# Suffix sums over key blocks taken as running sums on VectorE, with seven tail product pairs a head instead of ten, in a stick-breaking attention trunk

## The reference, cut to what matters

```python
def block(args):
    qi, i = args
    z = jnp.einsum('bhqd,bhkd->bhqk', qi, k).astype(jnp.float32) * scale
    q_pos = i * Q_BLOCK + jnp.arange(Q_BLOCK)
    strict = key_pos[None, :] < q_pos[:, None]
    log_1m = jnp.where(strict, jax.nn.log_sigmoid(-z), 0.0)
    tail = lax.cumsum(log_1m, axis=3, reverse=True) - log_1m
    a = jnp.where(strict, jnp.exp(jax.nn.log_sigmoid(z) + tail), 0.0)
    return jnp.einsum('bhqk,bhkd->bhqd', a.astype(v.dtype), v)
```

## Time and profile before

| | us |
|---|---|
| median of 3 runs | 760.4 (759.59 to 760.98) |
| the profiled execution's own time | 760.23 |
| its span, first to last instruction | 758.5 |

### The profile page before, as it was taken

How to read it: one execution, slowest core, us unless ns; L and a number is a source line. 1 busy time by engine, 2 the same in 40 slices (tenths; PEclk the granted TensorE clock), 3 DMA queues, 4 the chain that set the end, 5 groups by cost and what they waited for, 6 DMA issues and landing times.

```text
span 758.5 us, 9936 instructions
## 1 busy us (share of the span) xinstructions
PE 699.3 (92%) x3547; PEld 583.3 (77%) x3547; DVE 514.1 (68%) x563; ACT 413.8 (55%) x428; POOL 109.6 (14%) x112
## 2 busy tenths in 40 slices
PE   4999999979799999999999989999999999999920
PEld 3898888878688888888888948888888888888810
DVE  5878755665534326071544588999999999999927
ACT  6726675675442323131233337777777778777712
POOL 5000000000000000000000130333433443331120
PEclk9999999998899999999999999999999999999975
DMA  8552330000042232233476369999999999999444
GB/s 282 170 167 56 111 111 1 1 28 2 15 149 87 83 111 79 87 97 125 165 264 236 122 217 393 394 388 370 367 375 369 366 376 366 385 366 375 181 170 189
DMA packets 85169, 155.47 MB, mean 205 GB/s; under 512 B 6229, under 2 KB 37071, under 8 KB 84628
## 3 DMA queue, kind: packets, MB, share of 16 engines
q1 hardware_dynamic: 78452, 137.39, 51.2%
q0 software_dynamic: 6688, 17.69, 6.2%
HBM read 150.64 MB, written 12.58 MB: 215 GB/s over the span
## 4 chain that ended last, share of the span: by engine, by line
PE 83%; DVE 6%; ACT 5%; issue 3%; DMA 2%; POOL 1%; POOLq 0%; DVEq 0%; ACTq 0%
PE ps L481 24%; PE ps L482 24%; PE ps L483 24%; PE ps L1536 2%; PE ps L1276 1%; PE ps L1278 1%; DVE soft L1826 1%; PE ps L1593 1%; PE ps L1462 1%; PE ps L1562 1%; PE ps L1490 1%; DMA y_rows<-ye,y_col 1%; ACT log_in L911 1%; ACT log_in L909 1%; ACT soft_hi L917 1%
## 5 line engine op out<-in xcount | busy, mean ns | idle before, releaser
L454 DVE TENSOR_TENSOR ring_lo<-raw_a,ring_hi 128x2048 fp32r<-128x2048 f32 (+2 forms) x58 | 115.5, 1995 | 103.6 <-ACT ring_hi L448 103.6
L454 DVE TENSOR_TENSOR ring_lo<-raw,ring_hi 128x2048 fp32r<-128x2048 f32 x71 | 161.4, 2289 | 12.3 <-ACT ring_hi L448 11.0
L448 ACT ACTIVATE ring_hi<-raw 128x2048 fp32r<-128x2048 f32 x71 | 136.2, 1920 | 19.8 <-PE ps L483 19.8
L481 PE MATMUL ps<-hT_hi,ring_hi 128*128 128x512 f32 x288 | 114.3, 397 | 5.3 <-ACT attn L923 3.4
L448 ACT ACTIVATE ring_hi<-raw_a 128x2048 fp32r<-128x2048 f32 (+2 forms) x58 | 97.4, 1680 | 32.3 <-PE ps L483 32.3
L483 PE MATMUL ps<-hT_hi,ring_lo 128*128 128x512 f32 x288 | 113.1, 393 | 0.0
L482 PE MATMUL ps<-hT_lo,ring_hi 128*128 128x512 f32 x288 | 113.1, 393 | 0.0
L481 PE MATMUL ps<-ring_hi,xT_hi 128*128 128x512 f32 x240 | 94.8, 395 | 1.8 <-DVE xT_lo L2039 1.8
L483 PE MATMUL ps<-ring_hi,xT_lo 128*128 128x512 f32 x240 | 93.8, 391 | 0.0
L482 PE MATMUL ps<-ring_lo,xT_hi 128*128 128x512 f32 x240 | 93.7, 390 | 0.0
L481 PEld LDWEIGHTS ps<-hT_hi,ring_hi 128*128 128x128 f32 x288 | 54.6, 190 | 17.8 <-ACT attn L923 3.6
(11 more groups left out here) (347 smaller groups left out, 1230.4 us busy)
## 6 DMA issues: line engine op xcount, KB each, us to landing
raw<-in_w_down SPq DMA_DIRECT2D x25, 1024.0 KB
raw<-in_w_gate SPq DMA_DIRECT2D x47, 512.0 KB
raw<-in_w_up SPq DMA_DIRECT2D x47, 512.0 KB
raw_a<-in_w_in SPq DMA_DIRECT2D x15, 1024.0 KB
raw_a<-in_w_gate SPq DMA_DIRECT2D x17, 512.0 KB
raw_a<-in_w_up SPq DMA_DIRECT2D x17, 512.0 KB
raw_a<-in_w_down SPq DMA_DIRECT2D x7, 1024.0 KB
raw_a<-in_w_in SPq DMA_DIRECT2D x10, 512.0 KB, 7.5
```

What stands on the lines that cost most here:

```text
L448: act.activation(ring_hi[:, c[0] % SPLIT, 0:width], buf[:, 0:width], ACT.Copy).then_inc(hi_ready, 1)
L454: dve.tensor_tensor(ring_lo[:, s, 0:width], buf[:, 0:width], ring_hi[:, s, 0:width].bitcast(F32), ALU.subtract).then_inc(lo_ready, 1)
L481: pe.matmul(out_ap, l_hi, r_hi, start=start, stop=False, skip_group_check=True)
```

## The change

The suffix sum over key blocks is no longer made by products with ones. Behind `softplus(n)`, DVE adds the blocks up from the last to the first: block 2 takes block 3 (128 columns), block 1 takes block 2 (256), block 0 takes block 1 (384), each waiting for the one before (`link` puts a semaphore wait behind the instruction). With such running sums R, the tail of block s is triangle x R(s) + (ones - triangle) x R(s+1), so `tails` issues 4 + 3 = 7 pairs; the second matrix is `negrest`, and `negones` goes.

`log_in` goes, and `soft` and `soft_lo` are doubled, so the log is made in the buffer of the head's parity. The wait of `softplus` for the former head's tails and of `logarithm` for the former softplus goes; `soften` waits for the former head's tails instead. The order within a pair changes on all three engines: `softplus(2p+3)` is at the end of a pair on DVE, right behind `soft_low(2p+2)` and one projection's low part; the gate chunks are split in the middle of the next pair; `project_qk(5)` (24 matmuls of 512 columns) and `project_v(2)` (48 of 256) change places between `fill_a(0)` and `fill_b(0)`, and the first six of the 24 matmuls of `fill_b` go ahead of `values(2p+1)` (`CUT`). `values` of heads 6 and 7 go to banks 2 and 3, and the first gate to banks 6 and 7.

```diff
-    log_in = sb("log_in", [P, ZW], F32, "t", 0)
-    soft = sb("soft", [P, ZW], F32, "t", 5 * KB)
-    soft_lo = sb("soft_lo", [P, ZW], F32R, "t", 5 * KB)
+    soft = [sb(f"soft{b}", [P, ZW], F32, "t", 5 * b * KB) for b in range(2)]
+    soft_lo = [sb(f"soft_lo{b}", [P, ZW], F32R, "t", 5 * b * KB) for b in range(2)]
...
-    GATE_BANK = ((6, 2), (0, 1), (4, 5))
+    GATE_BANK = ((6, 7), (0, 1), (4, 5))
+
+    def value_bank(m):
+        return bank(7 if m < HEADS - 2 else m - 4)
...
                 act.wait_ge(z_ps, n + 1)
-                if n > 0:
-                    act.wait_ge(z_soft, n)
-                act.activation(log_in[:, :], scores(n), ACT.Abs).then_inc(act_c, 1)
+                buf = soft[n % 2]
+                act.activation(buf[:, :], scores(n), ACT.Abs).then_inc(act_c, 1)
...
             def soften(n):
                 act.wait_ge(z_soft, n + 1)
-                act.activation(soft_hi[:, :], soft[:, :], ACT.Copy).then_inc(soft_h, 1)
+                if n > 0:
+                    act.wait_ge(tail_ps, n)
+                act.activation(soft_hi[:, :], soft[n % 2][:, :], ACT.Copy).then_inc(soft_h, 1)
...
                 a, b = 2 * p, 2 * p + 1
+                soften(b)
                 weigh(a)
-                soften(b)
                 if p == 0:
-                    qk_hi(5, 6)
+                    v_hi_part(2, 6)
                 if p == 1:
                     qk_hi(6, 6)
+                    split_hi(act, K(C_MERGE))
                 if p == 2:
                     v_hi_part(3, 6)
+                    split_hi(act, K(C_MERGE + 1))
...
                 for sbk in range(TB):
-                    for jb in range(sbk, TB):
+                    for lhs, jb in ((negtri, sbk), (negrest, sbk + 1))[:TB - sbk]:
...
                 if p < HEADS // 2 - 1:
                     scores_pair(p + 1)
+                    fill_b(p, 0, CUT)
                 else:
-                    gate_part(KD // 2, KD).then_inc(chunk_used, 1)
+                    gate_half(0, 1, 0, None, 5, KD).then_inc(chunk_used, 1)
                 values(2 * p + 1)
-                fill_b(p)
+                if p < HEADS // 2 - 1:
+                    fill_b(p, CUT, KD)
...
+            dve.tensor_scalar(negrest[:, :], tri_f[:, :], -1.0, -1.0, ALU.mult, ALU.add).then_inc(consts_r, 1)
...
             def softplus(n):
                 dve.wait_ge(z_ln, n + 1)
-                if n >= 1:
-                    dve.wait_ge(tail_ps, n)
-                dve.scalar_tensor_tensor(soft[:, :], bank(3 * (n % 2), 3)[:, 0:ZW], 0.0, log_in[:, :],
-                                         ALU.max, ALU.add).then_inc(z_soft, 1)
+                buf = soft[n % 2]
+                link(dve.scalar_tensor_tensor(buf[:, :], bank(3 * (n % 2), 3)[:, 0:ZW], 0.0, buf[:, :],
+                                              ALU.max, ALU.add))
+                for sbk in (2, 1, 0):
+                    more = buf[:, ZOFF[sbk] + P:ZOFF[sbk] + ZN[sbk]]
+                    ins = dve.tensor_tensor(more, more, buf[:, ZOFF[sbk + 1]:ZOFF[sbk + 1] + ZN[sbk + 1]], ALU.add)
+                    if sbk > 0:
+                        link(ins)
+                ins.then_inc(z_soft, 1)
...
             cross_o(1)
             qk_lo(4, 6)
+            softplus(1)
             for p in range(HEADS // 2):
                 a, b = 2 * p, 2 * p + 1
-                softplus(b)
+                soft_low(b)
                 weight_hi(a)
-                soft_low(b)
                 weight_lo(a)
...
+                if p < HEADS // 2 - 1:
+                    softplus(b + 2)
                 value_lo(a)
                 value_lo(b)
```

More of the change, by code:

```diff
@@ L122, in build_trunk @@
     negtri = sb("negtri", [P, P], F32R, "const")
-    negones = sb("negones", [P, P], F32R, "const")
+    negrest = sb("negrest", [P, P], F32R, "const")
     rank_tri = sb("rank_tri", [P, P], BF16, "const")
@@ L954, in _ @@
                     soften(a + 2)
-                value_hi(a)
-                value_hi(b)
                 if p == 0:
-                    v_hi_part(2, 6)
+                    qk_hi(5, 6)
                 if p == 1:
@@ L962, in _ @@
                     logarithm(b + 2)
[L963 to L966, removed]
+                value_hi(a)
+                value_hi(b)
             act.preload_act_table_set("sigmoid_and_others")
@@ L974, in _ @@
                         after(act, K(C_MERGE + i, dp, PER_DP))
[L975 to L979, removed]
+                        act.activation(sig[:, i, :, :], gate_pair(i), ACT.Sigmoid).then_inc(g_sig, 1)
                 act.wait_ge(mg_ready, dp + 1)
@@ L1121, in _, with proj @@
                         ins.then_inc(hT_ps, 1)
-            def proj(b, wh, wl, o0, step):
-                for k in range(KD):
+            def proj(b, wh, wl, o0, step, k0=0, k1=KD):
+                for k in range(k0, k1):
                     o = o0 + k * step
@@ L1203, in cross_out, with project_qk @@
                 ins.then_inc(xo_ps, 1)
-            def project_qk(n, b):
+            def project_qk(n, b, k0=0, k1=KD):
                 wh, wl = chunk(K(C_PAIR[n // 2]))
-                proj(b, wh, wl, 1024 * (n % 2), P).then_inc(chunk_used if n % 2 else q_ps, 1)
+                ins = proj(b, wh, wl, 1024 * (n % 2), P, k0, k1)
+                if k1 == KD:
+                    ins.then_inc(chunk_used if n % 2 else q_ps, 1)
             def project_v(i, b):
@@ L1337, in _ @@
             project_qk(4, 6)
-            def gate_part(k0, k1):
-                wh, wl = chunk(K(C_MERGE))
-                for k in range(k0, k1):
-                    o = P + k * 256
-                    ins = three(pe, bank(GATE_BANK[0][1]), wh[:, o:o + P], wl[:, o:o + P], hT_hi[:, k, :], hT_lo[:, k, :],
-                                k == 0, k == KD - 1)
-                return ins
+            CUT = 2
             def fill_a(p):
@@ L1349, in fill_a @@
                     pe.wait_ge(qk_l, 5)
-                    project_qk(5, 6)
+                    project_v(2, 6)
                 if p == 1:
-                    pe.wait_ge(v_l, 3)
+                    pe.wait_ge(qk_l, 6)
                     project_qk(6, 6)
@@ L1798, in value_sum @@
                 dve.wait_ge(av_x, m + 1)
-                dve.tensor_tensor(sbT_f[rows, m // 2, :], bank(7)[rows, :], sbT_f[rows, m // 2, :], ALU.add).then_inc(av_sum, 1)
+                dve.tensor_tensor(sbT_f[rows, m // 2, :], value_bank(m)[rows, :], sbT_f[rows, m // 2, :], ALU.add).then_inc(av_sum, 1)
             cross_norm(0)
```

64 lines of the change are left out of this document (28 added, 36 removed).

## The result

The changed kernel takes 753.82 us (median of 5 runs, 751.12 to 755.46), beside 760.98 us (759.59 to 761.62) for the kernel before on the same chip: a ratio of 0.990 with a 95% interval of 0.987 to 0.993, that is 5.5 to 9.7 us less.

What follows compares the result with a forecast made beforehand. PE bounds the kernel (83% of the last chain), so a change counts where PE waits or its work shrinks. Full-clock savings of -9.8 us and +3.9 for clock falls give -5.9, 754.5 us; range 750.2 to 758.4.

Steps and rivals of the forecast that it cites:

- Tails and adds: Per head in the loop: tail products from 2.73 to 2.15 us; adds of 0.29, 0.42, 0.56 us, 1.35 with links.
- The chain: From z, the end of a pair's score products: first tails at 9.61 us; PE waits 2.9 there, 0.9 before second tails.
- The sum at full clock: Head loop without clock falls: -0.9 us before its first z, then +0.6, -5.5 and -4.0; together -9.8 us.
- The split: Gate chunk split in mid-pair (ACT 1.90, DVE 2.29 us) no longer holds up head 5; rival: something else does, chance 0.08.
- The fill ahead of the values: Six fill matmuls (1.38 us) before second head's values: only move the wait before first tails, yet cover late low weights.
- The clock: In the loop, three falls behind waits of about 2.9 us: net +3.8 to 3.9 us; rival: it stays up, chance 0.25.
- What is saved here moves everything behind it forward: Time saved in the head loop starts the following stage, full of PE work, earlier by the same amount.
- the prediction's own sign of being wrong: Among the signs named: the stage behind the head loop doesn't start earlier by the same amount.
- PEclk is below 1 in three stretches: Profile of the changed kernel: low TensorE clock in three stretches instead of two.

Runs made afterwards that it cites:

- e1: Changed kernel with its new order and buffers, but ten tail product pairs with ones and no adds: 748.73 us.
- e6: Changed kernel plus 20 products that nobody reads, in PE's wait before the first tails of each of three pairs: 752.82 us.
- e3: Changed kernel with both gate chunk splits put back at the end of the pair, behind the second head's logarithm: 764.16 us.
- e4: Kernel before with only the two gate chunk splits moved to the middle of their pair: 750.95 us.
- e2: Kernel before with the three adds, `negrest` and seven product pairs, in the old order with the old buffers: 767.78 us.
- e5: Changed kernel with all of `fill_b` behind the second head's values, none ahead of them: 753.27 us.
- e7: Changed kernel with a head's seven high-part products first, waiting for the high part alone, then the seven low-part ones: 752.12 us.
- r1: Changed kernel as it is, profiled a second time: 755.67 us in one run.
- e8: Changed kernel's order and buffers with ten product pairs, no adds, and the ten high-part products ahead of the ten low-part ones: 746.26 us.

## Why the prediction was right, and where it was not

754.5 was forecast, 753.82 came. The mechanism in the loop was right: the order gives, the sums take. That the total fits to 0.7 us is partly luck, as the last two points show. Step by step:

- **Tails and adds**: 2.15 us a head, and 0.291, 0.425, 0.560 us, as forecast. The rule of the Trainium skill, VectorE: DVE Perf Modes, section on the TRN2 errata, that each operation on SBUF pays a fixed latency, holds here: 128 columns took 0.291 us, not a third of the 0.560 that 384 took. Its cycle table gave 0.98 us for the three, an estimate, where they took 1.35 with their links. The same section says that this row of the table is too low, and for adds of this type gives 151 plus the columns, at 0.96 GHz; that is 0.291, 0.424 and 0.557 us, an estimate that these rows meet, and the prediction passed it over. (The second row is a copy, not an add; only the length of a link was taken from it.)
- **The chain**: tails 9.64 us behind z (forecast 9.61), PE idle 2.71 (forecast 2.9, though the forecast's own 9.61, less 6.8 of fills and values, is 2.8) and 0.63 (0.9). Right. e1's waits, 1.32 to 1.34, show that the adds are what makes the difference.
- **The sum at full clock**: e6 measures it. The first z in it is at 124.76, so -1.2 (forecast -0.9); then 24.57 us (24.7), 25.20 (24.7) and 25.84 (25.75), which is +0.5, -5.0 and -3.9. Together -9.6, where I had -9.8. The half microsecond above the forecast in the third period (25.20 for 24.7) stands beside a wait that I had not counted: there the values of head 4 wait 0.72 us for the low part of V, which DVE makes only after the low weights (170.44 in e6). e6 adds products to PE, but only where it waits.
- **The split**: e3 (+10.3 us) and e4 (-9.4 us) show that its place alone decides the sign of the change. That the split would have no price in the middle of the pair was right for ACT.
- **The fill ahead of the values**: "only moves this wait" was right. But I also had it cover the low weights of the second head, and said that PE would wait 1.4 us out without it. It does, and loses nothing, since it then waits that much less before the tails. The two sentences were one and the same 1.1 to 1.4 us.
- **The clock: mis-sized.** I charged three falls, behind the three waits of 2.9 us, the length of one at 5.2 us, 2.5 us each and +3.9 net. (The subtraction is off too: 2.5 less the 0.9 that is absorbed is 1.6, not 1.7.) The profile shows two falls of 3.41 us, one behind a 2.70 us wait and one behind the 2.18 before head 7. The third period is 25.81 us instead of e6's 25.20, and the last 27.26 instead of 25.84: +0.6 and +1.4, together the 2.05 us by which e6's loop ends earlier. Two things were off. First, "2.9 is nearer to 3.44 than to 0.79, so I let it fall three times": of twelve waits of 2.67 to 2.71 us in four profiles (the change, its two repeats, e3) five were followed by a fall. Around the waits of 3.4 to 6.3 us in the kernel before, e2 and e3 the clock was low each time. Behind shorter ones it fell at 1.66 (e4), 1.88 and 2.55 (e5), 1.98 and 2.33 (e2), 2.18 (the change), and in e7 at 1.18 with 0.27 behind it; it did not behind the three of 1.3 in e1, 1.55 in e5, 1.58, 1.58 and 1.65 in e2, 1.69 and 1.76 in e7 or 2.17 in e6. So no length parts the two cases up to 2.7 us; the chip's answer to the same wait differs from one execution to the next. Second, a fall costs less than its loss on PE, as the next wait absorbs it: in both repeats the fall behind the third 2.71 us wait left the last period at 25.8 us, because the wait for head 7 shrank from 2.17 to 0.6. That one I had nearly right, with 0.2. The Trainium skill, TensorE: Matmul & The Clock Gate, section on HAM oscillation, describes a loop whose waits of about 3 to 5 us bring the low clock back every time. The waits of 2.7 us here are shorter and brought it back in 5 of 12 cases, so that section did not bear out three falls, as the prediction has it.
- **"What is saved here moves everything behind it forward": failed.** By the prediction's own sign of being wrong, the stage behind the loop had to start earlier by the same amount; it starts 7.6 us earlier and the span is 6.1 us shorter, for the stage took 550.0 us where it had taken 548.5. In the thirteen profiles it lasts 548.3 to 548.6 us without a low stretch, 550.0 to 550.4 with one of 3.41 us, 551.9 with one of 6.83, and 553.2 to 553.6 with both, so 1.6 to 1.7 us for each 3.41. So -9.6 at full clock, +2.0 for the falls in the loop and +1.5 behind it make the -6.1 of the profiled span; I had +3.9 for the first and nothing for the second, and these nearly cancelled. That PEclk is below 1 in three stretches, as forecast, is luck in the same way: two lie in the loop and the third behind it.

**What stays open.** A stretch that begins between 409 and 413 us (at 420 in e3) stands in all seven profiles of kernels with the sums in the new order, and in none of the other six. PE is recorded fully busy there, in kernels with and without the stretch, and the 32 products of 20 columns stand at that place or just ahead of it in all of them. The second stretch behind the loop in r1 and e6, at 447 us, comes with a wait of 1.80 and 1.85 us on PE; the other eleven profiles have the same wait, 1.46 to 1.86 us, without one. The time at which the stage starts does not decide it alone: e4 starts it at 200.59 us without one, e6 and e7 at 200.37 and 200.30 with. Nor do the two groups of kernels surely part. Two of e1's six runs, of which there is no trace, took 752.45 and 753.32 us at a mean granted clock of 0.973, where the other four had 0.978 to 0.981, and two of the thirteen runs of the kernel before beside it took 762.60 and 763.05 us at 0.970, where its profiles had 0.972. And the two fastest of e6's six runs, 750.45 and 750.53 us, have a span of 748.7 at 0.981, which is e6's loop end of 200.37 with 548.3 us behind it, so most likely no low stretch at all. I have no trace that shows one kernel both with and without it. That the wider range of the changed kernel's runs (751.1 to 755.5) comes from the number of low stretches fits the profiles, but was only argued.

## What to carry to other kernels

When one edit bundles a new order and a new algorithm, try the parts alone: here one gave 11.6 us and the other took 4 to 5 back. Trading products on TensorE for adds on VectorE lost time here, in either order, because TensorE waited for the chain that the adds lengthened; look at which engine waits where they meet. That it would pay where TensorE is the later one was not run. Here a separate wait for the operand that is ready first brought another 2.5 us (e8 beside e1) without any work saved; in the kernel with the sums (e7 beside the change) it brought nothing clear of the spread. Keep long operations that nobody waits for, like a weight split, out of the stretch between a logarithm and the softplus that follows it.

## What the runs showed of the hardware

- Between 96 and 713 us, every stretch at 0.50 in all thirteen profiles lasted 3.41 or 6.83 us, whatever the wait ahead of it (added up from slices of 0.8 us).
- The same code gave one, two or three of them in the loop in three profiled executions, where the kernel before gave the same two in both of its own. Waits of 1.18 to 2.71 us on PE were followed by one in some places and not in others.
- One near 412 us came with PE recorded busy 2.00 of 2.00 us (the window at 413.50 above), behind 32 products of 20 columns, and each 3.41 us at 0.50 in that stage cost 1.6 to 1.7 us.
- Adds of float32 on DVE took 0.291, 0.425 and 0.560 us for 128, 256 and 384 columns.
